# Latent attention layer: the probabilities' halves and the next tile's scaling queued between two halves of the filling, and the first head's units ahead of the second gate

## The chip, the cores and the metric

One core of a Trainium2 chip runs the whole program in one launch. The metric is the device time of one execution in microseconds (us). The kernel before takes 2921.37 us, the median of 3 runs (2921.25 to 2922.08).

## The reference

A decoder trunk of four residual layers on x of 1024 tokens by 1024 features, in float32: gated linear attention, multi-head latent attention (MLA), stick-breaking attention, gated linear attention, then a last RMSNorm. Only the MLA layer is touched by the change:

```python
proj = h @ w_in                      # c_q 256, c_kv 128, k_rope 64, gate g 2048
q = (rmsnorm(c_q) @ w_uq)            # 16 heads x (128 + 64 rotary)
kv = (rmsnorm(c_kv) @ w_ukv)         # 16 heads x (128 key + 128 value)
for i in range(8):                   # query tiles of 128 rows, all heads
    s = (q_nope[i] @ k_nope[:k_end].T + q_rope[i] @ k_rope[:k_end].T) * scale
    p = softmax(where(causal, s, -inf))          # k_end = 128 * (i + 1)
    o[i] = p @ v[:k_end]
y = (o * silu(g)) @ w_out            # 2048 -> 1024, added to x
```

## The kernel before, in words

**Numbers.** Every matrix product is made of three float16 products: each operand is split in a high half (ScalarE: a scaled copy to f16) and a low half (VectorE: the value less its high half). The stream x stays transposed in on-chip memory (xT, eight blocks of 128 features by 1024 tokens).

**Order.** A layer writes one list of items, `build_items` (L1047). Each engine's program goes through this list and issues its own share of every item (L454 to L480), so the list is the order of work on TensorE (PE), VectorE (DVE), ScalarE (ACT), GpSimd (POOL) and the SyncE queue (SP) alike. An engine waits at a semaphore for what it needs and everything of its own behind that waits with it.

**Items of one tile.** The 16 heads have 8 tiles each, t = 0 to 127, tile i of a head being i+1 blocks of 128 keys wide. For a tile t:

- `s` (L1154, PE): the scores, five products per 512 columns and one for the mask, in PSUM pair t mod 2. It waits for the low half of tile t-2 (L1164), which last used that pair.
- `m` (L1277 DVE, L1378 ACT): the row maximum of the scores, its negative, and on ACT the exponential with the row sum.
- `d` (L1290, DVE): the reciprocal of the row sum and the scaling of the probabilities in place.
- `t` (L1181, PE): i+1 transposes back to the PSUM pair. They wait for `d`.
- `e` (L1389 ACT, L1301 DVE): the high half of the transposed probabilities, then the low half.
- `pv` (L1188, PE): 3(i+1) products with the values. After every fourth tile DVE multiplies the result with the gate (yt, L1315), ACT makes its high half (L1403), POOL its low half (L1450).

In the list before, tile t+1's scores stand first and the filling stands behind `e`:

```python
main += [("s", t + 1)] if t < last else []
main += [("d", t)]
main += [("m", t + 1)] if t < last else []
main += [("t", t), ("e", t), ("gap", 1)]
main += [("pv", t - 1)] if t else []
```

**The filling.** At each ("gap", 1) the function `weave` (L45) puts in items of other work, in proportion to the cost of `pe_cost` (L996; 4 per product of 512 columns). A weave covers eight tiles: tile 7 of the head h-1 and tiles 0 to 6 of head h. Its filling is, in this order: the units of head h+1 (`head_items`, L1029), for an even h+1 first two rotary units of queries (qr) with their `rope` steps, then qn, qn, kn, kn, v, v; for h of 4 and more four output units (x), each cut in four parts; for h of 1 to 14 two gate units (g), each cut in four parts. So there are weaves with rotary units (h odd) and plain ones (h even). From head 4 on a weave's filling costs 528 (h odd) or 480 (h even).

What a finished unit leaves to other engines: qn, kn and v an ACT high half and a DVE low half (L443, L450); qr three DVE instructions (L1258, L1262 twice), a POOL sum, an ACT and a DVE half and 8 small DMAs by SP (L1478); x one DVE addition (L399); g the chain `gz` (L256): an ACT copy, a DVE clamp (L274), three ACT functions (L263, L265, L267), and at the item `g2`, behind the next unit, a DVE product (L280). `place_gates` (L1085) keeps `gz` at its place in the list here. The ACT half of a v unit waits until the products `pv` of the head before the last are done (L1360). Every slab of weights has one ACT and one DVE instruction for its halves (L182, L188), which `finish_items` (L142) puts ahead of the first unit of the slab before. Units take the PSUM banks 5, 6, 7 in turn, and a unit waits until the bank's last one is read.

**The start of the layer.** Behind the latent units come the gate of head 0, the gate of head 1 with the two `rope` steps of the keys in it, the units of head 0, and then `s` 0 and `m` 0. A `rope` step of queries makes SP issue 8 DMAs, which move the rotary halves to other partitions; `s` 0 waits for all 16 (L1161).

Of the kernel before, what the change touches and what calls it, by code (L numbers as in the profile page):

```python
# [44 lines left out]
def weave(main, filler, cost):  # L45

    total_weight = sum(item[1] for item in main if item[0] == "gap")
    total_cost = sum(cost(item) for item in filler)
    out, k, weight, spent = [], 0, 0, 0
    for item in main:  # L50
        if item[0] != "gap":
            out.append(item)
            continue
        weight += item[1]
        while k < len(filler) and (spent * total_weight < weight * total_cost):
            out.append(filler[k])
            spent += cost(filler[k])
            k += 1
    return out + filler[k:]
# [434 lines left out]
class StickBreaking:  # L494
# [112 lines left out]
    def build_items(self, w_in, w_out):  # L607
        L = self.L
        filler = L.cut(self.projections(0, w_in), ("q", "k", "v", "g"))
        first_gate = next(i for i, it in enumerate(filler) if it[0] == "part" and L.units[it[1]][0] == "g") - 1  # L610
        items = [("start",)] + filler[:first_gate] + [("z", 0), ("lh", 0), ("ll", 0), ("z", 1)]
        filler = filler[first_gate:]

        main = []
        for p in range(self.PAIRS):
            for i, step in enumerate(self.attention(p)):
                if i == self.SHIFT:
                    items += weave(main, filler, lambda it: it[0] in ("u", "part"))
                    filler = L.cut(self.projections(p + 1, w_in), ("q", "k", "v", "g")) if p + 1 < self.PAIRS else []
                    main = []  # L620
                main += step

        last = []
        for k in range(KD):
            last += L.slab(w_out[k], 1024, [("x", (k, c, True)) for c in range(2)], [5, 6, 7])
        early, last = L.open_early(L.cut(last, ("x",)), 2)
        items += weave(main, early, lambda it: it[0] == "part")
        items += [("pv", self.PAIRS * len(self.STEPS) - 1)] + last
        L.finish_items(items)
# [293 lines left out]
class LatentAttention:  # L923
# [123 lines left out]
    def build_items(self):  # L1047
        L = self.L
        latent = [self.add_slab(self.w["latent"][b], 1024, [("c", (b, c)) for c in range(2)]) for b in range(3)]
        items = [("start",)] + latent[0] + latent[1] + latent[2][:2] + [("sums", 0)] + latent[2][2:] + [("latent", 0)]  # L1050
        keys = self.add_slab(self.w["latent"][3], 1024, [("kr", (0, c)) for c in range(2)])
        items += keys[:2] + [("sums", 1)] + keys[2:] + [("latent", 1)]
        items += self.gate_items(0)
        ahead = self.gate_items(1)
        at = next(i for i, it in enumerate(ahead) if it[0] == "u") + 1
        items += ahead[:at] + [("rope", 0), ("rope", 1)] + ahead[at:] + self.head_items(0)
        last = MLA_HEADS * TT - 1
        items += [("s", 0), ("m", 0)]
        main, filler = [], []
        for t in range(last + 1):  # L1060
            h, i = divmod(t, TT)
            if i == 0:
                if h + 1 < MLA_HEADS:
                    filler += self.head_items(h + 1)
                if h >= self.GROUP:
                    filler += self.out_items(h // self.GROUP - 1, h % self.GROUP)
                if 1 <= h < MLA_HEADS - 1:
                    filler += self.gate_items(h + 1)
            if i == TT - 1:
                items += weave(main, L.cut(filler, ("x", "g")), self.pe_cost)  # L1070
                main, filler = [], []
            main += [("s", t + 1)] if t < last else []
            main += [("d", t)]
            main += [("m", t + 1)] if t < last else []
            main += [("t", t), ("e", t), ("gap", 1)]
            main += [("pv", t - 1)] if t else []
        items += [it for it in main if it[0] != "gap"]
        tail = []
        for part in range(4):
            tail += self.out_items(MLA_HEADS // self.GROUP - 1, part)  # L1080
        early, tail = L.open_early(L.cut(tail, ("x",)), 3)
        items += early + [("pv", last)] + tail
        L.finish_items(self.place_gates(items))
# [1098 lines left out]
```

How the kernel before makes its waits and increments, by code:

```python
    def load_slab(self, sp, s):  # L160
        if s >= len(self.slabs):
            return
        dram, cols = self.slabs[s]
        if s >= self.NLOAD:
            sp.wait_ge(self.w_lo_done, s - self.NLOAD + 1)
            sp.wait_ge(self.w_hi_done, s - self.NLOAD + 1)
        sp.dma_start(self.wf[s % self.NLOAD][:, 0:cols], dram).then_inc(self.w_loaded[s % self.NLOAD], 16)
# [8 lines left out]
    def act_w(self, act, s):  # L176
        cols = self.slabs[s][1]
        act.wait_ge(self.w_loaded[s % self.NLOAD], 16 * (s // self.NLOAD + 1))
        if s >= self.NSPLIT:
            act.wait_ge(self.acc_ready, self.last_unit_of[s - self.NSPLIT])
            act.wait_ge(self.w_lo_done, s - self.NSPLIT + 1)
        act.activation(self.w_hi[s % self.NSPLIT][:, 0:cols], self.wf[s % self.NLOAD][:, 0:cols],
                       ACT.Copy, scale=W_SCALE).then_inc(self.w_hi_done, 1)
# [1 line left out]
    def dve_w(self, dve, s):  # L185
        cols = self.slabs[s][1]
        dve.wait_ge(self.w_hi_done, s + 1)
        dve.scalar_tensor_tensor(out=self.w_lo[s % self.NSPLIT][:, 0:cols],
                                 in0=self.wf[s % self.NLOAD][:, 0:cols], scalar=W_SCALE,
                                 in1=self.w_hi[s % self.NSPLIT][:, 0:cols],
                                 op0=ALU.mult, op1=ALU.subtract).then_inc(self.w_lo_done, 1)
# [1 line left out]
    def wait_unit(self, eng, n):  # L193
        eng.wait_ge(self.acc_free[self.units[n][3]], self.turn[n])
# [86 lines left out]
    def wait_done(self, eng, n):  # L282
        eng.wait_ge(self.done, self.order.index(n) + 1)
```

## Time and profile before

| | |
|---|---|
| median of 3 runs | 2921.37 us |
| the profiled execution's own time | 2920.31 us |
| its span, first to last instruction | 2918.6 us |
| busy, whole span | PE 85%, PEld 49%, DVE 52%, ACT 44%, POOL 14% |
| mean granted TensorE clock | 0.944 |
| the latent layer | about 535 to 1580 us of the span |
| its attention, first scores to last transposes | 665 to 1532 us |

PE is busy over 85% of the span and every other engine for about half of it or less, so the time is read as the work of PE plus what PE waits for. The chain that ended last shows only the last normalization, 20 us at the end, and says nothing of this layer; the waits and the order of time inside the layer do.

### The profile page before, as it was taken

The numbers are of one execution on the slowest core, as the hardware profiler recorded it, in microseconds if no ns is written. First come the engines' busy times: TensorE is split into PE (matmuls) and PEld (weight loads), VectorE is DVE, ScalarE is ACT, GpSimd is POOL, SyncE is SP. The second block draws the span as 40 slices with busy tenths as digits, with TensorE's granted clock in tenths as the row PEclk, the third lists the DMA queues.
The fourth block names the chain that finished last, engine by engine and source line by source line (L and its number), as shares of the span: only waits on it lengthen the run. The fifth ranks groups of instructions, "written<-read, shape, count | busy, mean of one in ns | idle before, by whom it ended". The sixth has DMA issues, their size and how long they took to land. (4 is left out here: it accounts for less than half of the span.)

```text
span 2918.6 us, 43195 instructions
## 1 busy us (share of the span) xinstructions
PE 2487.2 (85%) x17616; PEld 1425.6 (49%) x17616; DVE 1518.8 (52%) x2167; ACT 1283.1 (44%) x1937; POOL 411.3 (14%) x300
## 2 busy tenths in 40 slices
PE   4999988686888988988886899999998779999977
PEld 1667643233545554554553455444454335665543
DVE  5455453455565565555554455555555434455543
ACT  3433332243443443344433477777777423334321
POOL 2000001220000001010003122222222230000001
PEclk9999999898999999999998899999999989999998
DMA  2111100101011010010100111111111001111002
GB/s 88 37 37 37 38 29 30 51 20 28 21 31 33 21 35 27 31 33 21 41 15 29 51 51 51 44 51 38 44 42 47 22 23 37 37 37 37 30 29 72
DMA packets 43032, 107.87 MB, mean 37 GB/s; under 512 B 7986, under 2 KB 13362, under 8 KB 42836
## 3 DMA queue, kind: packets, MB, share of 16 engines
q1 hardware_dynamic: 42836, 105.11, 11.7%
q8 instruction: 141, 2.31, 0.3%
q14 instruction: 55, 0.45, 0.0%
HBM read 84.11 MB, written 4.19 MB: 30 GB/s over the span
## 5 line engine op out<-in xcount | busy, mean ns | idle before, releaser
L1387 ACT ACTIVATE mla_prob<-psum,mla_neg_top 128x128 f32<-128x128 f32 (+7 forms) x128 | 94.5, 738 | 369.1 <-DVE mla_neg_top L1288 340.8
L219 PE MATMUL psum<-h_hi,gla_w_hi 128*128 128x512 f16 (+1 forms) x544 | 212.5, 391 | 41.7 <-DVE h_lo L377 41.7
L888 POOL TENSOR_TENSOR sb_al<-sb_zc,sb_ah 128x256 f16<-128x256 f32 (+2 forms) x96 | 166.2, 1731 | 419.8 <-ACT sb_ah L852 419.8
L220 PE MATMUL psum<-h_lo,gla_w_hi 128*128 128x512 f16 (+1 forms) x544 | 211.7, 389 | 0.0
L221 PE MATMUL psum<-h_hi,gla_w_lo 128*128 128x512 f16 (+1 forms) x544 | 210.9, 388 | 0.0
L1305 DVE TENSOR_TENSOR mla_pt_lo<-psum,mla_pt_hi 128x128 f16<-128x128 f32 (+7 forms) x128 | 97.0, 758 | 195.2 <-ACT mla_pt_hi L1395 195.2
L235 PE MATMUL psum<-gla_w_hi,h_hi 128*128 128x128 f16 x1024 | 173.8, 219 | 0.0
L236 PE MATMUL psum<-gla_w_lo,h_hi 128*128 128x128 f16 x1024 | 173.6, 219 | 0.0
L237 PE MATMUL psum<-gla_w_hi,h_lo 128*128 128x128 f16 x1024 | 173.6, 219 | 0.0
L1185 PE MATMUL psum<-mla_ident,mla_prob 128*128 128x128 f32 x576 | 90.1, 285 | 94.2 <-DVE mla_prob L1300 94.1
L219 PE MATMUL psum<-h_hi,sb_w_hi 128*128 128x512 f16 x384 | 151.1, 394 | 22.4 <-DVE h_lo L377 22.4
L399 DVE SCALAR_TENSOR_TENSOR xT<-psum,xT 128x512 f32<-128x512 f32 x112 | 77.1, 689 | 178.9 <-PE psum L221 178.8
L1284 DVE TENSOR_REDUCE mla_top<-psum 128x1 f32<-128x128 f32 (+7 forms) x128 | 96.7, 755 | 106.4 <-PE psum L1179 106.3
L220 PE MATMUL psum<-h_lo,sb_w_hi 128*128 128x512 f16 x384 | 151.1, 393 | 0.0
L221 PE MATMUL psum<-h_hi,sb_w_lo 128*128 128x512 f16 x384 | 150.7, 392 | 0.0
L219 PE MATMUL psum<-h_hi,mla_w_hi 128*128 128x512 f16 x320 | 124.8, 390 | 29.8 <-DVE h_lo L377 24.3
L759 DVE TENSOR_TENSOR sb_Ll<-sb_Lf,sb_Lh 128x256 f16<-128x256 f32 (+2 forms) x96 | 96.9, 1009 | 90.2 <-ACT sb_Lh L844 90.2
L1450 POOL TENSOR_TENSOR mla_y_lo<-mla_yt,mla_y_hi 128x512 f16<-128x512 f32 x32 | 37.0, 1156 | 688.9 <-ACT mla_y_hi L1403 688.9
L220 PE MATMUL psum<-h_lo,mla_w_hi 128*128 128x512 f16 x320 | 124.6, 389 | 0.0
L1185 PEld LDWEIGHTS psum<-mla_ident,mla_prob 128*128 128x128 f32 x576 | 66.9, 143 | 117.4 <-DVE mla_prob L1300 111.6
L221 PE MATMUL psum<-h_hi,mla_w_lo 128*128 128x512 f16 x320 | 124.2, 388 | 0.0
L829 ACT ACTIVATE sb_Lf<-sb_zc 128x256 f32<-128x256 f32 (+2 forms) x96 | 80.8, 842 | 95.6 <-DVE sb_zc L753 95.6
(316 smaller groups left out, 6951.3 us busy)
## 6 DMA issues: line engine op xcount, KB each, us to landing
sb_wf<-in_sb_in SPq DMA_DIRECT2D x32, 512.0 KB, 3.7
gla_wf<-in_gla_v SPq DMA_DIRECT2D x16, 512.0 KB, 3.5
gla_wf<-in_gla_g SPq DMA_DIRECT2D x16, 512.0 KB, 3.5
gla_wf<-in_gla_out SPq DMA_DIRECT2D x16, 512.0 KB, 3.4
mla_wf<-in_mla_gate SPq DMA_DIRECT2D x16, 512.0 KB, 3.4
mla_wf<-in_mla_out SPq DMA_DIRECT2D x16, 512.0 KB, 3.5
xT<-in_x_T SPq DMA_DIRECT2D x8, 512.0 KB, 6.5
gla_wf<-in_gla_q SPq DMA_DIRECT2D x8, 512.0 KB, 3.5
```

What stands on the lines that cost most here:

```text
L219: pe.matmul(out, wh[:, w], act_hi[:, k, tok], start=(i == 0), stop=False)
L220: pe.matmul(out, wh[:, w], act_lo[:, k, tok], start=False, stop=False)
L221: mm = pe.matmul(out, wl[:, w], act_hi[:, k, tok], start=False, stop=(i == last))
L235: pe.matmul(out, act_hi[:, k, tok], wh[:, w], start=(i == 0), stop=False)
L236: pe.matmul(out, act_hi[:, k, tok], wl[:, w], start=False, stop=False)
L237: mm = pe.matmul(out, act_lo[:, k, tok], wh[:, w], start=False, stop=(i == last))
L759: dve.tensor_tensor(self.Ll[s % 2][:, :, off:HALF], self.Lf[s % 2][:, :, off:HALF], self.Lh[s % 2][:, :, off:HALF], ALU.subtract).then_inc ...
L888: pool.tensor_tensor(self.al[s % 2][:, :, off:HALF], self.zc[s % 4][:, :, off:HALF], self.ah[s % 2][:, :, off:HALF], ALU.subtract).then_in ...
L1185: mm = pe.transpose(self.pair(t)[:, j * P:(j + 1) * P], self.prob[t % 2][:, j * P:(j + 1) * P], self.ident[:])
L1284: dve.reduce_max(self.top[:, k], self.pair(t)[:, 0:w], AX_X).then_inc(self.top_ready, 1)
L1305: dve.tensor_tensor(self.pt_lo[t % 2][:, 0:w], self.pair(t)[:, 0:w], self.pt_hi[t % 2][:, 0:w], ALU.subtract).then_inc(self.ptl_ready, 1)
L1387: act.activation(self.prob[t % 2][:, 0:w], self.pair(t)[:, 0:w], ACT.Exp, bias=self.neg_top[:, k], scale=self.SCALE, accum_out=self.total[ ...
```

## The change

The units of head 0 stand ahead of the second gate, the key's `rope` steps stand in the first gate, and `d` 0 stands behind `m` 0. In the tile loop `d` of a tile moves one tile ahead of its transposes, and the one gap becomes two, with `e` of this tile and `d` of the next between them. The number of gaps of a weave goes from 8 to 16, each worth half as much. No instruction is added or removed.

```diff
-        items += self.gate_items(0)
-        ahead = self.gate_items(1)
+        ahead = self.gate_items(0)
         at = next(i for i, it in enumerate(ahead) if it[0] == "u") + 1
-        items += ahead[:at] + [("rope", 0), ("rope", 1)] + ahead[at:] + self.head_items(0)
+        items += ahead[:at] + [("rope", 0), ("rope", 1)] + ahead[at:] + self.head_items(0) + self.gate_items(1)
         last = MLA_HEADS * TT - 1
-        items += [("s", 0), ("m", 0)]
+        items += [("s", 0), ("m", 0), ("d", 0)]
         main, filler = [], []
         for t in range(last + 1):
...
-            main += [("s", t + 1)] if t < last else []
-            main += [("d", t)]
-            main += [("m", t + 1)] if t < last else []
-            main += [("t", t), ("e", t), ("gap", 1)]
+            main += [("s", t + 1), ("m", t + 1)] if t < last else []
+            main += [("t", t), ("gap", 1), ("e", t)]
+            main += [("d", t + 1)] if t < last else []
+            main += [("gap", 1)]
             main += [("pv", t - 1)] if t else []
```

## Rows read from the trace of the kernel before

**Rows 1.** Busy time of the attention stretch: PE, PEld, DVE, ACT, POOL, clock, DMA

```profile
666.00:1544.00 878.00, 750.04 (x5375) 444.28 (x5373) 503.12 (x971) 355.46 (x681) 62.57 (x46) 0.95 0.09 28
```

**Rows 2.** Waits of PE, 666 to 1532 us: total, times, longest

```profile
PE psum L1185 <- DVE mla_prob L1300: 94.1, 50, 4.1
PE psum L1173 <- DVE mla_pt_lo L1305: 25.8, 27, 2.3
```

**Rows 3.** Timeline of PE at head ends: start, us, idle before, releaser

```profile
1037.01 0.48 PE L1185 MATMUL psum<-mla_ident,mla_prob 128*128 128x128 f32 x1 [4.08 <-DVE mla_prob L1300]
...
1047.14 0.44 PE L1185 MATMUL psum<-mla_ident,mla_prob 128*128 128x128 f32 x2 [1.60 <-DVE mla_prob L1300]
...
1076.90 0.38 PE L1173 MATMUL psum<-mla_kn_hi,mla_qn_hi 128*128 128x512 f16 x1
...
1085.75 1.09 PE L1185 MATMUL psum<-mla_ident,mla_prob 128*128 128x128 f32 x8 [1.21 <-DVE mla_prob L1300]
...
1091.09 0.27 PE L1173 MATMUL psum<-mla_kn_hi,mla_qn_hi 128*128 128x256 f16 x1
...
1093.31 0.33 PE L1185 MATMUL psum<-mla_ident,mla_prob 128*128 128x128 f32 x1 [1.46 <-DVE mla_prob L1300]
...
1103.09 0.44 PE L1185 MATMUL psum<-mla_ident,mla_prob 128*128 128x128 f32 x2 [3.57 <-DVE mla_prob L1300]
```

**Rows 4.** Busy time by stretches of 2 us, columns as in rows 1

```profile
1104.00:1106.00 2.00, 1.66 (x5) 0.59 (x5) 0.42 (x1) 0.67 (x3) 0.47 (x1) 0.51 0.05 12
```

**Rows 5.** Timeline of PE, SP and DVE at the layer's start

```profile
629.46 0.53 PE L219 MATMUL psum<-h_hi,mla_w_hi 128*128 128x512 f16 x1 [2.48 <-DVE mla_w_lo L188]
...
653.28 0.62 SPq L1478 DMA_DIRECT2D mla_qr_stack<-mla_st_hi  x1
...
662.96 0.59 SPq L1478 DMA_DIRECT2D mla_qr_stack<-mla_st_lo  x1
...
665.97 0.29 DVE L1284 TENSOR_REDUCE mla_top<-psum 128x1 f32<-128x128 f32 x1 [8.63 <-PE psum L1179]
```

**Rows 6.** Timeline of DVE at a plain head end

```profile
1082.81 1.09 DVE L1305 TENSOR_TENSOR mla_pt_lo<-psum,mla_pt_hi 128x896 f16<-128x896 f32 x1 [2.08 <-ACT mla_pt_hi L1395]
...
1084.41 0.42 DVE L274 TENSOR_SCALAR mla_gate_tmp<-mla_silu_g 128x512 f32<-128x512 f32 x1
...
1084.94 0.75 DVE L1300 TENSOR_SCALAR mla_prob<-mla_prob,mla_inv_total 128x1024 f32<-128x1024 f32 x1
...
1088.11 1.22 DVE L1305 TENSOR_TENSOR mla_pt_lo<-psum,mla_pt_hi 128x1024 f16<-128x1024 f32 x1 [2.03 <-ACT mla_pt_hi L1395]
1089.25 1.22 DVE L188 SCALAR_TENSOR_TENSOR mla_w_lo<-mla_wf,mla_w_hi 128x1024 f16<-128x1024 f32 x1
1090.39 0.68 DVE L450 SCALAR_TENSOR_TENSOR mla_qn_lo<-psum,mla_qn_hi 128x512 f16<-128x512 f32 x1
```

**Rows 7.** Timeline of ACT at the same head end

```profile
1084.87 0.63 ACT L263 ACTIVATE mla_gate_tmp<-mla_gate_tmp 128x512 f32<-128x512 f32 x1 [1.54 <-DVE mla_gate_tmp L274]
...
1087.07 1.01 ACT L1395 ACTIVATE mla_pt_hi<-psum 128x1024 f16<-128x1024 f32 x1
1087.97 1.05 ACT L182 ACTIVATE mla_w_hi<-mla_wf 128x1024 f16<-128x1024 f32 x1
1088.92 1.21 ACT L443 ACTIVATE mla_qn_hi<-psum 128x512 f16<-128x512 f32 x2
...
1098.69 1.08 ACT L443 ACTIVATE mla_v_hi<-psum 128x512 f16<-128x512 f32 x2 [3.66 <-PE psum L1203]
```

**Rows 8.** Timeline of DVE at a head end with rotary units

```profile
1029.55 0.68 DVE L1258 SCALAR_TENSOR_TENSOR mla_rt<-psum,mla_cos 128x512 f32<-128x512 f32 x1
1030.25 1.39 DVE L1262 SCALAR_TENSOR_TENSOR mla_rt<-psum,mla_sin 64x512 f32<-64x512 f32 x2
```

**Rows 9.** Timeline of ACT, tile 5 of a plain head

```profile
1073.04 1.01 ACT L1387 ACTIVATE mla_prob<-psum,mla_neg_top 128x896 f32<-128x896 f32 x1 [1.91 <-DVE mla_neg_top L1288]
...
1074.04 0.80 ACT L1395 ACTIVATE mla_pt_hi<-psum 128x768 f16<-128x768 f32 x1
```

## The prediction

> **What bounds the kernel now.** I read the page first (PE busy 85% of the span, no other engine much above half), then the busy time by stretches, then PE's waits, then the order of time around the longest of them. The attention stretch is 878 us long with PE busy for 750 [rows 1]. Nearly all the missing time is two waits: transposes that wait for the scaled probabilities (`t` for `d`), 94.1 us, and scores that wait for the low half (`s` for `e`), 25.8 us [rows 2]. The timeline shows where. Inside a head PE runs from item to item with no gap. It stands at head ends: 1.21, 1.46 and 3.57 us at a plain one, 4.08 and 1.60 us at one with rotary units [rows 3]. The reader is to see that `d` is late only because DVE serves it behind everything the filling left to it. After such a stand the granted clock is 0.51 of full, the level of 1.2 GHz, for some stretches [rows 4]; over the attention it is 0.95 [rows 1]. At the layer's start DVE waits 8.63 us for the first scores, while SP issues 16 DMAs from 653.28 to 663.55 [rows 5].
>
> **The start.** The rotary units' DMAs now run beside the second gate. Before, PE waited until 629.46 for the second gate's weight halves [rows 5] and then worked 10.4 us on it (48 products of 0.216). Now it takes the rotary units there, but head 0's own weight halves stand behind both gate chains on ACT, so PE stands some 5.6 us, at about 631 to 636.5. Behind that, rotary drains, halves and ropes on DVE run to about 645, `rope` 2 is ready at about 643.7 instead of 653.28, and its DMAs are issued until 654 and landed at 655.5. PE finishes the gate at 656.5 and starts the scores, 8.6 us before 665.1. The gate's chain (0.6 + 0.4 + three functions) is now ahead of the first exponential on ACT, so the first transposes come at 660.5 instead of 667.5. I take **-6.5 us**; bounds -8.6 (all of DVE's wait) and -3 (the stand at 631 turned into slow clock for the gate).
>
> **The loop, inside a head.** `e` now waits for the first half of the filling. For wide tiles PE has filling (3.3 us) and products (up to 1.2 us) to cover exponential, high half and low half; where only x parts and their one DVE addition lie in the first half, that cover holds and I cost it at nothing. If it were gone, `e` would cost PE its own 0.7 to 1.2 us per tile. Two places do not hold.
> (a) Gate chain in the first half. With cost 480 in 16 gaps of 30, gap 13 reaches for 390; the first gate unit ends at 384, so its chain `gz` goes into that same, odd gap, ahead of `e` of tile 5. Odd gaps are the ones before `e`. With 528 (33 a gap) gap 13 is full at 432, where the unit ends, and `gz` falls in gap 14, harmless. In the plain heads ACT finishes exp(6) at 1074.04 and now does the chain before the 0.80 us high half [rows 9]: 0.55 copy, 0.4 clamp, 2.0 functions put it at 1077.0 and the low half's end at 1078.7. PE, which started scores 7 at 1076.9 [rows 3], stands **1.8 us**, in six weaves (h = 4 to 14).
> (b) With rotary units, the gate slab's weight halves (1.05 ACT, 1.22 DVE, as in [rows 6, 7]) fall in gap 5 ahead of `e` of tile 1: 1.3 us.
>
> **A plain head end.** d(7) follows e(6) at once, at 1083.8; before, a gate product and the clamp stood between [rows 6]. Transposes 7 start 0.95 earlier, of the 1.21 of [rows 3]. But the clamp and so ACT's chain are 0.8 later: chain end and exp(0) at 1087.85. Ahead of hi(7) now stand the weight half (0.95 net) and two qn halves (1.2) [rows 7]: hi(7) is done at 1090.9 instead of 1088.0. DVE has its weight half, qn_lo, gate product and qn_lo ahead of e(7), which ends at 1093.0 instead of 1089.3 [rows 6]. Scores 1, which must wait for e(7), started at 1091.1 [rows 3]; now at 1093.0, transposes 0 end at 1093.8 against 1093.5. So **the stand of 1.46 becomes one of 3.4 at another semaphore, +0.3 us**. Next, the v halves on ACT wait for products 7 [rows 7], and hi(0), e(0), d(1) are now queued behind them: products 7 end at 1099.2, e(0) at 1101.35, transposes 1 end at 1102.5 against 1103.37, a stand of 2.1 for one of 3.57. That is 0.9 us won. The clock, however: the 3.4 us stand is as long as those that end at 0.5, and now the slow stretch lies on kn, v and x parts that release products 7. I charge 1.8 there and take back the 1.7 that the x parts pay now (their stretch at 0.51 [rows 4]). Result -0.8, then +1.8 for (a): **+1.0 us**. At h = 4, 8, 12 the fourth x part waits for POOL's low half of the head just finished, which is later than before behind d(1), a weight half and yt: +1.9 more, **+2.9**.
>
> **A rotary head end.** DVE is the bound there: each rotary unit leaves it 2.1 us (0.68 + 1.39) [rows 8]. Now w_lo, drain, gate product and drain stand before e(7), which ends at 1035.0; scores 1 start there and transposes 0 end at 1035.8, against 1037.3 [rows 3]. Then ropes, qn and kn halves reach e(0) at 1041.6, products 7 end at 1042.2 (a v unit waited 1.8 for its bank), transposes 1 end at 1043.4, or 1044.1 at the slow clock, against 1047.4 [rows 3]. So 3.3 us won, less 1.3 for (b): **-2.0 us**.
>
> **Heads 0 to 3 and 15** (no x, or only x): head 0 is bound by the chain through e, and three units in odd gaps put a half of 0.6 us into it, less one that is hidden: +1.5. Heads 1 and 3: the two rotary units fall in two different gaps, so e(7) stands behind one drain only: -3 each. Heads 2 and 15: 0.
>
> **Sum** against the profiled 2920.3: -6.5 + 1.5 - 2 x 3 - 5 x 2.0 + 3 x 1.0 + 3 x 2.9 = -9.3, so 2911. The median of the runs is 1.1 above the profiled execution: **2912 us**.
>
> The trace and a rule side by side: d(0) at rotary head ends starts only when DVE has ended the qn half in front of it, 4.08 us late for PE [rows 3]. The Trainium skill says the same as a general rule, that ACT's and DVE's queues are strictly in order while PE's can pull weight loads forward (TensorE: Matmul & The Clock Gate, Architectural detail). It speaks against this change, since it moves `e`, too, behind half of the filling; its time is the second rival's.
>
> **Rivals.**
> 1. The waits really go. For: 94.1 us wait for `d` alone, and `d` is now queued a whole tile earlier; it ends the slow clock too. Against: at head ends DVE and ACT, not the place of `d`, set the pace, and `e` joins the queue. If two thirds of 94.1 went, with 10 us of clock and the start: 2921 - 63 - 10 - 6 = 2842; if a third, 2921 - 31 - 5 - 6 = 2879. Chance 0.12.
> 2. Slower: the low half behind the filling. Place: the 14 head ends with filling ahead of e(7). Price: scores 1 wait for e(7) as at the plain head above, and the stand's slow clock falls on the units that release products 7 without the old slow stretch going; then each plain end costs 1.7 more and each rotary end 2 more than I took. 2912 + 7 x 1.7 + 7 x 2 = 2938. It decides from the point where the two stands after transposes 7 together exceed the old ones (5.0 plain, 5.7 rotary). Chance 0.27.
> 3. The loop nets nothing and only the start counts, 2914.9, or the start's gain goes as well because the DMAs, issued one by one, still end last: 2921. Chance 0.13 for the first, 0.05 for the second.
> My own case has 0.43.
>
> **Chances.** About 0.2% (5.8 us) is what a measurement of this kernel can tell from no change. My case, 2898 to 2920 by itself, is faster by more than that in about 0.33 of its 0.43; rival 1 always; half of the first part of rival 3. Slower by over 0.2% is rival 2 with a little of my case. Faster 0.52, same 0.21, slower 0.27. The range leaves out the far part of rival 1 and the end of rival 2: 2884 to 2936.
>
> **What would show it.** Right: PE's wait at the transposes falls from 94.1 to under 25, while its wait at the scores (for pt_lo) rises from 25.8 to 70 or more; first scores at 656 to 657; a stand of 2 or so before scores 7 in even heads from 4 on, none in odd ones; stands before scores 1 of 3 to 4 us, and the clock at half behind them. Wrong: a total of both waits under 60 us, a clock of 0.97 or more over the attention, or first scores later than 660.

## The result, and the profile after

The changed kernel takes 2926.14 us (median of 19 runs, 2922.43 to 2931.58) against 2919.99 us of the kernel before on the same chip (19 runs, 2912.11 to 2924.63). The ratio is 1.0024 with a 95% interval of 1.0018 to 1.0031: it is **slower by 0.24%**, where the forecast was 2912 us, faster by 0.3%. The profiled execution of after took 2923.05 us with a span of 2921.3 us. PE is busy for 85% of it, DVE for 52%, ACT for 44%, POOL for 14%, and the mean granted clock is 0.944: at this grain the page cannot be told from that of before. Of all runs in this document one, of experiment 9 at 6461.6 us, is more than twice as long as the others of its kernel and is left out of its ratio.

PE's waits can. The view is PE's waits between 655 and 1537 us of the kernel after, up to the last transposes as in [rows 2]: total, times, longest (L1172 is the first product of the scores, L1184 the transposes).

```profile
PE psum L1172 <- DVE mla_pt_lo L1304: 120.2, 65, 4.3
PE psum L1184 <- DVE mla_prob L1299: 9.6, 17, 3.1
```

Against [rows 2], 94.1 us at the transposes became 9.6, and 25.8 us at the scores became 120.2. The sum went from 119.9 to 129.8: for the 84.5 us that PE no longer waits for the scaling it waits 94.4 us more for the low half. The busy row of the attention, columns as in [rows 1], has the same clock of 0.95; PE is busy for 84.5% of it, against 85.4% in [rows 1]:

```profile
664.00:1550.00 886.00, 748.74 (x5364) 448.86 (x5365) 496.66 (x963) 350.30 (x674) 57.67 (x46) 0.95 0.09 27
```

**Where in the layer.** The latent layer, from its first Newton step (the first DVE step of its first normalization, L303; 540.26 us before, 536.76 after) to that of the next layer, is 1060.6 us long against 1051.6 before, +8.9. The way from that first step to the first transposes is 122.4 against 127.3, -4.9. The rest is by head: each head's time below is taken from the start of the transposes of tile 7 of the head before it to the start of its own (head 0 from its first transposes; PE's timeline has both).

| head | before, us | after, us | difference | forecast |
|---|---|---|---|---|
| 0 | 36.39 | 40.44 | +4.05 | +1.5 |
| 1 | 51.50 | 52.76 | +1.26 | -3 |
| 2 | 44.32 | 49.32 | +5.00 | 0 |
| 3 | 53.46 | 53.49 | +0.03 | -3 |
| 4, 8, 12 | 56.22, 56.00, 55.97 | 57.06, 60.51, 59.42 | +8.80 in all | +8.7 |
| 6, 10, 14 | 55.75, 55.74, 55.73 | 56.99, 56.29, 57.98 | +4.04 in all | +3 |
| 5, 7, 9, 11, 13 | 60.29, 60.30, 60.17, 60.25, 60.17 | 57.63, 57.62, 58.62, 57.88, 58.57 | -10.86 in all | -10 |
| 15 | 40.78 | 42.25 | +1.47 | 0 |

So heads 4 to 14 came out at +2.0 where the prediction's terms give +1.7, and heads 0 to 3 at +10.3 where they give -4.5. The same is seen in the waits. PE's waits up to 866 us, some 11 us into head 4 as the table counts it, first of the kernel before (from 665 us), then of the kernel after (from 655 us):

```profile
PE psum L1185 <- DVE mla_prob L1300: 19.5, 15, 2.7
PE psum L1173 <- DVE mla_pt_lo L1305: 16.7, 11, 2.3
```

```profile
PE psum L1172 <- DVE mla_pt_lo L1304: 45.6, 21, 4.3
PE psum L1184 <- DVE mla_prob L1299: 4.2, 5, 3.1
```

Both waits together are 36.2 us before and 49.8 us after in the first quarter of the layer. In the rest they are 83.7 before (119.9 less 36.2) and 80.0 after (129.8 less 49.8).

**The head ends after.** PE's timeline (start, us, idle before it, releaser) in one rotary head (its end of [rows 3] and scores 3 inside it) and in the plain head behind it (its end, and scores 7 inside it, the last line):

```profile
1037.48 0.28 PE L1172 MATMUL psum<-mla_kn_hi,mla_qn_hi 128*128 128x256 f16 x1 [3.47 <-DVE mla_pt_lo L1304]
...
1051.17 0.39 PE L1172 MATMUL psum<-mla_kn_hi,mla_qn_hi 128*128 128x512 f16 x1 [1.23 <-DVE mla_pt_lo L1304]
...
1084.48 1.09 PE L1184 MATMUL psum<-mla_ident,mla_prob 128*128 128x128 f32 x8 [0.27 <-DVE mla_prob L1299]
...
1092.88 0.28 PE L1172 MATMUL psum<-mla_kn_hi,mla_qn_hi 128*128 128x256 f16 x1 [2.90 <-DVE mla_pt_lo L1304]
...
1102.26 0.34 PE L1172 MATMUL psum<-mla_kn_hi,mla_qn_hi 128*128 128x384 f16 x1 [2.21 <-DVE mla_pt_lo L1304]
...
1106.35 0.61 PE L219 MATMUL psum<-mla_y_hi,mla_w_hi 128*128 128x512 f16 x1 [1.48 <-POOL mla_y_lo L1449]
...
1137.07 0.39 PE L1172 MATMUL psum<-mla_kn_hi,mla_qn_hi 128*128 128x512 f16 x1 [1.75 <-DVE mla_pt_lo L1304]
```

These are the stands the prediction walked through, at its places: 3.47 before scores 1 at a rotary end (3 to 4 forecast), 1.23 before scores 3 (1.3), 2.90 before scores 1 at a plain end (3.4), 2.21 behind the v halves (2.1), 1.48 for POOL's low half (1.9), and 1.75 before scores 7 (1.8), where the gate's chain lies ahead of the high half. DVE at the plain end, to be laid beside [rows 6]:

```profile
1083.67 0.76 DVE L1299 TENSOR_SCALAR mla_prob<-mla_prob,mla_inv_total 128x1024 f32<-128x1024 f32 x1
...
1088.67 1.23 DVE L188 SCALAR_TENSOR_TENSOR mla_w_lo<-mla_wf,mla_w_hi 128x1024 f16<-128x1024 f32 x1 [2.92 <-ACT mla_w_hi L182]
1089.82 0.68 DVE L450 SCALAR_TENSOR_TENSOR mla_qn_lo<-psum,mla_qn_hi 128x512 f16<-128x512 f32 x1
...
1091.62 1.21 DVE L1304 TENSOR_TENSOR mla_pt_lo<-psum,mla_pt_hi 128x1024 f16<-128x1024 f32 x1
```

Two executions are laid side by side by the start of transposes 7, 1085.75 before [rows 3] and 1084.48 here, since earlier parts of them differ too. The scaling now lets transposes 7 start after a stand of 0.27 us instead of 1.21, the 0.95 forecast. The low half of tile 7, which before stood ahead of the weight half, now stands behind it: it ends 8.35 us behind the start of transposes 7 (1092.83) instead of 3.58 (1089.33), 4.8 us later. The exchange can be read off these four lines.

**The clock** behind such a stand, by stretches of 2 us (columns as in [rows 1]), at this plain end and behind the longest stand of head 2:

```profile
786.00:788.00 2.00, 2.00 (x6) 0.76 (x5) 1.03 (x2) 0.63 (x1) 0.23 (x1) 0.50 0.00 0
...
1094.00:1096.00 2.00, 2.00 (x11) 1.11 (x10) 0.58 (x2) 0.89 (x3) 0.00 (x0) 0.50 0.00 0
...
1104.00:1106.00 2.00, 0.87 (x3) 0.00 (x0) 1.02 (x3) 1.54 (x4) 0.86 (x1) 0.50 0.52 131
```

At 0.50 of full the granted clock is the 1.2 GHz level. The prediction charged 1.8 us for a new slow stretch behind scores 1 and took back 1.7 for the old one of [rows 4], on the x parts. In this head both came: the stretch from 1104 us is at 0.50 still. Over the six plain heads of this execution, only head 10 has what was charged, the new one without the old. Heads 8 and 14 have both, and heads 4, 6 and 12 have only the one on the x parts.

### The profile page after: what moved, and what is told of

It reads as the page before. It is cut to its first block and busy times, and to the rows that moved or that the text cites. A ratio compares the mean times of both kernels' runs of the same rounds, so it can differ in the third digit from the quotient of the medians.

```text
span 2921.3 us, 43195 instructions
## 1 busy us (share of the span) xinstructions
PE 2483.2 (85%) x17616; PEld 1430.1 (49%) x17616; DVE 1513.6 (52%) x2167; ACT 1280.1 (44%) x1937; POOL 407.2 (14%) x300
## 5 line engine op out<-in xcount | busy, mean ns | idle before, releaser
L235 PE MATMUL psum<-gla_w_hi,h_hi 128*128 128x128 f16 x1024 | 173.8, 219 | 0.0
L1172 PE MATMUL psum<-mla_kn_hi,mla_qn_hi 128*128 128x512 f16 (+1 forms) x192 | 65.0, 338 | 120.7 <-DVE mla_pt_lo L1304 120.2
L829 ACT ACTIVATE sb_Lf<-sb_zc 128x256 f32<-128x256 f32 (+2 forms) x96 | 80.8, 842 | 94.4 <-DVE sb_zc L753 94.4
L766 DVE TENSOR_TENSOR sb_zc<-sb_zc,psum 128x256 f32<-128x256 f32 (+2 forms) x96 | 91.2, 950 | 52.3 <-PE psum L689 52.3
```

The lines of the kernel that those rows point to most:

```text
L235: pe.matmul(out, act_hi[:, k, tok], wh[:, w], start=(i == 0), stop=False)
L766: dve.tensor_tensor(zc, zc, net.psum[:, 2:4, off:HALF], ALU.subtract).then_inc(self.arg_ready, 1)
```

## The experiments

All runs are compared with the kernel before on their own chip, whose median was between 2919.5 and 2920.3 us. Diffs are against the changed kernel unless it is said otherwise.

**1 and 2. Which half of the change costs.** The changed start with the loop of before, and the loop alone with the start of before.

```diff
-        items += [("s", 0), ("m", 0), ("d", 0)]
+        items += [("s", 0), ("m", 0)]
...
-            main += [("s", t + 1), ("m", t + 1)] if t < last else []
-            main += [("t", t), ("gap", 1), ("e", t)]
-            main += [("d", t + 1)] if t < last else []
-            main += [("gap", 1)]
+            main += [("s", t + 1)] if t < last else []
+            main += [("d", t)]
+            main += [("m", t + 1)] if t < last else []
+            main += [("t", t), ("e", t), ("gap", 1)]
```

> The changed start of the layer with the tile loop of before. Theory L (the start wins about 6 us, the loop loses about 14, ten of them in the weaves of heads 0 to 3): first transposes 6 us earlier relative to the layer's start, all later head periods as before, time ratio to before 0.998 (2914 against 2920). Rival R (the start's gain is given back by slow clock and standing in head 0, the loop loses only 6 or 7, evenly): ratio 1.000.

```diff
-        ahead = self.gate_items(0)
+        items += self.gate_items(0)
+        ahead = self.gate_items(1)
...
-        items += ahead[:at] + [("rope", 0), ("rope", 1)] + ahead[at:] + self.head_items(0) + self.gate_items(1)
+        items += ahead[:at] + [("rope", 0), ("rope", 1)] + ahead[at:] + self.head_items(0)
```

> The changed tile loop with the start of before. Theory L: 2920 + 14 = 2934, ratio 1.0047. Rival R: 2920 + 7 = 2927, ratio 1.0024, the same as the whole change.

Measured: the start alone 2916.88 us, ratio 0.9996 [0.9987, 1.0006]; the loop alone 2932.89 us, 1.0052 [1.0038, 1.0066]. The loop alone costs 0.52%, about 15 us. The start alone cannot be told from no change, though in its profile the way to the first transposes is 122.42 us against 127.26, the same 4.8 us as after. Its profiled heads are those of before within 0.5 us each, so the loop is where the loss is. On the loop theory L's 1.0047 lies in the interval and the rival's 1.0024 does not; on the start it is the other way round, for L's 0.998 lies outside and the rival's 1.000 inside.

**3 and 7. Which heads.** The loop of before for heads 0 to 3 and the new one behind them, and the complement. Both have the changed start.

```diff
-        items += [("s", 0), ("m", 0), ("d", 0)]
+        items += [("s", 0), ("m", 0)]
...
-            main += [("s", t + 1), ("m", t + 1)] if t < last else []
-            main += [("t", t), ("gap", 1), ("e", t)]
-            main += [("d", t + 1)] if t < last else []
-            main += [("gap", 1)]
+            if (t + 1) // TT < 4:
+                main += [("s", t + 1), ("d", t), ("m", t + 1)]
+                main += [("t", t), ("e", t), ("gap", 1)]
+            else:
+                main += [("s", t + 1)] if t < last else []
+                main += [("d", t)] if t + 1 == 4 * TT else []
+                main += [("m", t + 1)] if t < last else []
+                main += [("t", t), ("gap", 1), ("e", t)]
+                main += [("d", t + 1)] if t < last else []
+                main += [("gap", 1)]
```

> The changed kernel, but the tiles up to the end of head 3 keep the old order and one gap; from tile 7 of head 3 on the new order. Theory L: the heads 0 to 3 give back their 10 us, time 2926 - 10 = 2916, ratio to before 0.9987 (start -6, heads 4 to 15 +3.5). Rival R: the loss is in every head, so at most a quarter of it comes back: 2924, ratio 1.0015.

```diff
-            main += [("s", t + 1), ("m", t + 1)] if t < last else []
-            main += [("t", t), ("gap", 1), ("e", t)]
-            main += [("d", t + 1)] if t < last else []
-            main += [("gap", 1)]
+            if (t + 1) // TT < 4:
+                main += [("s", t + 1), ("m", t + 1)]
+                main += [("t", t), ("gap", 1), ("e", t)]
+                main += [("d", t + 1), ("gap", 1)]
+            else:
+                main += [("s", t + 1)] if t < last else []
+                main += [("d", t)] if t + 1 > 4 * TT else []
+                main += [("m", t + 1)] if t < last else []
+                main += [("t", t), ("e", t), ("gap", 1)]
```

> The complement of the run with the old loop in heads 0 to 3: the new loop only up to the end of head 3, the old one behind it. Theory L: the heads 0 to 3 lose 10 us and heads 4 to 15 are as before: start -5, +10, time 2925, ratio to before 1.0017. Rival R (loss spread evenly): 2918, ratio 0.9993.

Measured: with the new order in heads 4 to 15 only, 2919.77 us, 1.0005 [0.9996, 1.0013], between the two numbers expected, so by itself it settles nothing. With the new order in heads 0 to 3 only, 2925.3 us, 1.0021 [1.0012, 1.0031], where the rival had 0.9993. Its heads 0 to 3 take 39.93, 53.54, 50.10 and 53.45 us, 197.0 in all against 185.7 before, and its heads from 5 on are those of before within 0.1 us. Head 4, where the two orders meet, takes 1.6 us more than before. Less the start alone (0.9996), the new order costs 0.25% (7.3 us) in four heads and 0.09% (2.6 us) in the twelve others. Each is the difference of two ratios that are known to about 0.1%, so the 0.25% is clear of zero and the 0.09% is not. The loss lies in the main in the quarter of the heads that has the least filling.

**4. The gate's chain.** A `gz` that falls between `t` and `e` is held back and put behind the next `d`.

```diff
-        L.finish_items(self.place_gates(items))
+        L.finish_items(self.place_gates(self.defer_gates(items)))
...
+    def defer_gates(self, items):
+        out, held, inside = [], [], False
+        for item in items:
+            if item[0] == "t":
+                inside = True
+            if inside and item[0] == "gz":
+                held.append(item)
+                continue
+            out.append(item)
+            if inside and item[0] in ("d", "pv"):
+                inside = False
+                out += held
+                held = []
+        return out + held
```

> The changed kernel, but a gate chain that falls into the first half of the filling is issued behind the low half and the next scaling. It touches head 2 (a stand of 4.1 us before scores 6 and a slow clock behind it) and heads 4, 6, ..., 14 (a stand of 1.75 us each before scores 7). Theory L: 4.5 + 6 x 1.75 = 15 us less than the changed kernel, 2911, ratio to before 0.997. Rival (the next thing in the queue is just as late, so that other stands take over half of it): 2918, ratio 0.9995.

Measured: 2912.37 us, 0.9978 [0.9969, 0.9986]; the chain's place is worth 0.46% (1.0024 less 0.9978), about 13 us. Theory L's 0.997 lies in the interval and the rival's 0.9995 outside. Scores 6 of head 2 in PE's timeline, first of the kernel after, then of this one:

```profile
785.77 0.53 PE L1172 MATMUL psum<-mla_kn_hi,mla_qn_hi 128*128 128x512 f16 x1 [4.14 <-DVE mla_pt_lo L1304]
```

```profile
786.37 0.39 PE L1187 MATMUL psum<-mla_kn_hi,mla_qn_hi 128*128 128x512 f16 x1 [1.20 <-DVE mla_pt_lo L1319]
```

Head 2 falls from 49.32 to 44.71 us (44.32 before), and the six plain heads from 4 to 14 together from 348.3 to 341.0: heads 8 and 12 by 3.1 and 2.0, and head 4 is 1.0 longer. The stand of 1.75 before scores 7 is gone there. ACT's timeline of the kernel after shows the 4.14 us being made:

```profile
780.34 0.90 ACT L1386 ACTIVATE mla_prob<-psum,mla_neg_top 128x768 f32<-128x768 f32 x1 [3.98 <-DVE mla_neg_top L1287]
...
781.23 0.59 ACT L261 ACTIVATE mla_silu_g<-psum 128x512 f32<-128x512 f32 x1
782.31 0.63 ACT L263 ACTIVATE mla_gate_tmp<-mla_gate_tmp 128x512 f32<-128x512 f32 x1 [0.49 <-DVE mla_gate_tmp L274]
782.97 0.63 ACT L265 ACTIVATE mla_gate_tmp<-mla_gate_tmp 128x512 f32<-128x512 f32 x1
783.63 0.63 ACT L267 ACTIVATE mla_gate_tmp<-mla_gate_tmp 128x512 f32<-128x512 f32 x1
784.17 0.69 ACT L1394 ACTIVATE mla_pt_hi<-psum 128x640 f16<-128x640 f32 x1
```

From the exponential's end the high half is 2.9 us away, of which the copy, the clamp's round trip and three functions take all. The low half ends at 785.7 and the scores start. The exponential's own 3.98 us of idle time says that ACT was not short of time; the order hurt.

**8. The rotary steps.** As experiment 4, but `rope` items are held and not `gz`.

```diff
-            if inside and item[0] == "gz":
+            if inside and item[0] == "rope":
```

(against experiment 4)

> The changed kernel, but a rope step that falls into the first half of the filling is issued behind the low half and the next scaling. In heads 1 and 3 the low half of tile 1 waited for the second rotary half on ACT, which waited for POOL, busy with the low half of the finished head: a stand of 4.3 us before scores 3. Theory L: these two stands shrink to under 2 us and the rotary head ends of heads 5 to 13 win up to 1 us each: 2926 - 2 x 3 - 5 x 0.7 = 2916.5, ratio to before 0.9988. Rival (the next unit's drain takes the place of the rope): 2925, ratio 1.0017.

Measured: 2925.69 us, 1.0023 [1.0013, 1.0033], which holds the rival's 1.0017 and not the theory's 0.9988: nothing is won. Scores 3 and scores 4 of head 1 in PE's timeline, first after, then here:

```profile
721.11 0.61 PE L1172 MATMUL psum<-mla_kn_hi,mla_qn_hi 128*128 128x512 f16 x1 [4.29 <-DVE mla_pt_lo L1304]
...
727.59 0.39 PE L1172 MATMUL psum<-mla_kn_hi,mla_qn_hi 128*128 128x512 f16 x1 [0.93 <-DVE mla_pt_lo L1304]
```

```profile
719.75 0.39 PE L1187 MATMUL psum<-mla_kn_hi,mla_qn_hi 128*128 128x512 f16 x1 [1.76 <-DVE mla_pt_lo L1319]
...
726.43 0.39 PE L1187 MATMUL psum<-mla_kn_hi,mla_qn_hi 128*128 128x512 f16 x1 [2.64 <-DVE mla_pt_lo L1319]
```

2.5 us go at scores 3 and 1.7 come back at scores 4. Heads 1 and 3 take 50.62 and 52.76 us, 2.1 and 0.7 less than after, and other heads of this profile give it back (head 4 alone takes 2.4 us more). So this run does not show that the rotary steps cost the kernel anything. The stand of 4.29 us itself is read from three engines in turn, POOL, ACT and DVE of the kernel after:

```profile
716.36 1.15 POOL L1449 TENSOR_TENSOR mla_y_lo<-mla_yt,mla_y_hi 128x512 f16<-128x512 f32 x1 [9.55 <-ACT mla_y_hi L1402]
717.47 1.26 POOL L1438 TENSOR_TENSOR mla_rt<-mla_rt 128x512 f32<-128x512 f32 x1
```

```profile
718.77 0.63 ACT L1376 ACTIVATE mla_st_hi<-mla_rt 128x512 f16<-128x512 f32 x1 [1.79 <-POOL mla_rt L1438]
```

```profile
719.43 0.69 DVE L1275 TENSOR_TENSOR mla_st_lo<-mla_rt,mla_st_hi 128x512 f16<-128x512 f32 x1 [3.16 <-ACT mla_st_hi L1376]
...
720.64 0.41 DVE L1304 TENSOR_TENSOR mla_pt_lo<-psum,mla_pt_hi 128x256 f16<-128x256 f32 x1
```

The rotary sum stands behind a y_lo on POOL, its high half behind that on ACT, its low half behind that on DVE, and the tile's own low half, 0.41 us of work, behind all of them.

**5 and 6. Both ahead of the filling.** If the low half was made late by being moved, it should go back ahead of the filling, with the new place of `d` kept: first with a gap between `e` and `d`, then with none.

```diff
-            main += [("t", t), ("gap", 1), ("e", t)]
+            main += [("t", t), ("e", t), ("gap", 1)]
```

> The changed kernel, but the halves of the probabilities stand ahead of all filling again, as before; only the next tile's scaling stays in the middle. Theory L (it is the low half behind the filling that costs): PE's wait at the scores falls from 120 to about 30 us; the scaling in the middle is still behind the drains of the first half, so part of the old wait at the transposes stays, 50 us or more. Time 2898, ratio to before 0.9925. Rival (the wait only belongs to whatever is queued last on DVE at a head end, so that the sum of the two waits stays about 120): time 2915, ratio 0.9985.

```diff
-            main += [("t", t), ("gap", 1), ("e", t)]
+            main += [("t", t), ("e", t)]
```

> The changed kernel, but halves and next scaling both stand ahead of one whole gap of filling. Theory L: nothing of the softmax waits behind filling of its own tile; wait at the scores about 30 us, at the transposes under 15; new stands of 1.5 to 2.8 us at kn, v or x units whose bank is drained late. Plain head ends 2.7 us shorter than before, rotary ones 4.4, start 5: 2920 - 5 - 7 x 2.7 - 7 x 4.4 = 2865, ratio 0.981. Rival (same sum of waits, moved to the banks of the units): 2915, ratio 0.9985.

Measured: 2905.65 us, 0.9956 [0.9944, 0.9969], and 2893.31 us, **0.9919 [0.9906, 0.9933]**, the fastest kernel of this study and faster than before and after. The theory's 0.9925 and 0.981 went too far, the rival's 0.9985 not far enough. In experiment 5 PE waits 31.0 us at the scores and 63.4 at the transposes (655 to 1545 us of its profile), as its theory said (about 30, and 50 or more): with the low half back ahead of the filling, PE's long wait for it is gone. PE's waits from 655 to 1535 us of the second kernel:

```profile
PE psum L1172 <- DVE mla_pt_lo L1304: 42.9, 37, 2.3
PE psum L219 <- DVE mla_w_lo L188: 23.7, 13, 2.8
PE psum L235 <- issue: 17.9, 15, 2.5
PE psum L219 <- POOL mla_y_lo L1449: 15.1, 4, 4.1
PE psum L219 <- issue: 12.0, 10, 1.8
PE psum L1184 <- DVE mla_prob L1299: 9.6, 17, 3.1
```

The two old waits are 52.5 us together, where before and after have 120 and 130. But 69 us of waits stand in places that had under 6 before: for weight halves, for POOL's low half, and "issue", where the trace names no releaser. One of each in PE's timeline:

```profile
1091.00 0.61 PE L219 MATMUL psum<-mla_y_hi,mla_w_hi 128*128 128x512 f16 x1 [4.14 <-POOL mla_y_lo L1449]
...
1133.77 0.39 PE L219 MATMUL psum<-mla_cq_hi,mla_w_hi 128*128 128x512 f16 x1 [2.75 <-DVE mla_w_lo L188]
...
1143.92 0.22 PE L235 MATMUL psum<-mla_w_hi,mla_ckv_hi 128*128 128x128 f16 x1 [2.46 <-issue]
```

A unit stands where the other engines have not caught up with the units before it; the product at L235 is the first of a v unit, and that it waits for its bank is argued from its place. The layer is 1030.8 us long, 20.8 less than before.

Most of the waits did not go but moved, as the rival said of their sum, though not of the time. From the first transposes to transposes 7 of head 15, all of PE's waits together are 118.5 us here, 125.1 before and 139.3 after. That stretch is 15.0 us shorter than before: PE stands still for 9.2 us less, and is busy for 732.1 us instead of 737.9, at a granted clock of 0.96 instead of 0.95. The start gives another 6.1 us.

**9. The products ahead of the filling too.** Would `pv` ahead of the gap release the v halves and POOL's y_lo sooner?

```diff
-            main += [("t", t), ("gap", 1), ("e", t)]
+            main += [("t", t), ("e", t)]
             main += [("d", t + 1)] if t < last else []
+            main += [("pv", t - 1)] if t else []
             main += [("gap", 1)]
-            main += [("pv", t - 1)] if t else []
```

> Halves and next scaling ahead of all filling, as in the run e6_e_d_first, and the products of the tile before ahead of the filling as well. Theory (what is left at head ends are drains that wait for the last tile's products: the v halves on ACT, and the POOL half that x parts need): the waits of PE for POOL fall from 15 us to under 7 and those put down to issue at kn, v and x units from 30 to under 15; heads 4 to 14 shorter by 1 to 2 us each; time 2880, ratio to before 0.987. Rival (the filling has to lie directly ahead of the products, else the scores of the next tile meet DVE with a full queue): 2893 or more, ratio 0.992 or more.

Measured: 2917.3 us, 0.9993 [0.9983, 1.0002]: the theory's 0.987 fell, and the rival (0.992 or more) stands. PE's waits for POOL went from 15.1 us to 2.7, as the theory said, but those put down to issue rose from 29.9 to 64.5, where it had under 15. Plain heads take 53.5 us, where experiment 6 has 57.1 to 57.3 in heads 4, 8 and 12 and 53.1 in heads 6, 10 and 14; rotary heads take 62.6, 3 to 4 more than there and 2.4 more than before. PE's and then ACT's timeline at a rotary end:

```profile
1043.94 0.27 PE L235 MATMUL psum<-mla_w_hi,mla_ckv_hi 128*128 128x128 f16 x1 [7.34 <-issue]
```

```profile
1041.50 0.63 ACT L1376 ACTIVATE mla_st_hi<-mla_rt 128x512 f16<-128x512 f32 x1 [2.48 <-POOL mla_rt L1438]
```

The last y_lo of the finished head has moved ahead of the rotary sums on POOL (it ends at 1040.25, and ACT's half waits for the sum behind it), and PE stands 7.34 us at a unit behind them. That the one causes the other is argued from the order, since the trace names no releaser there.

**10. What the start is worth.** Experiment 6 with the start of before (its `d` 0 still behind `m` 0).

> The run e6_e_d_first with the start of before. If the start's gain of about 5 us does not depend on the loop behind it: 2893 + 5 = 2898, ratio to before 0.9935. If it is given back in this loop: 2893, ratio 0.992.

Measured: 2904.2 us, 0.9948 [0.9935, 0.9960], so beside the better loop the start is worth 0.0029 of 2920, some 8.5 us (the two intervals leave room for 3 to 14), and the loop of experiment 6 by itself wins 0.52%, as much as the changed loop by itself costs. Of the two numbers expected, 0.9935 is at the edge of the interval and 0.992 outside. In the profiles the way to the first transposes is 121.20 us with it and 128.25 without, 7.1 us. Beside the changed loop it is worth 0.28% (1.0052 less 1.0024) and beside the old one 0.04%, with an interval from a gain of 0.13% to a loss of 0.06%.

## Why the prediction was wrong

**The step that failed** is the term for the first heads: "head 0 is bound by the chain through e ... +1.5", "Heads 1 and 3 ... -3 each", "Heads 2 and 15: 0". For heads 0 to 3 it gave -4.5; they came out at +10.3 in the profile, a miss of 14.8 us, and by timed runs at +7.3 (experiments 1 and 7), 11.8 off, of the 16.3 between the forecast's -9.3 and the measured +7.0 (0.24% of 2920). The terms were set down without a walk through the new order, while heads 4 to 14, which had one, came out within 0.3 us in sum. (The same order ran in them in the profiles of experiments 2 and 3, at +3.6 and +3.3 us against before.)

Under it lies a reading that was too wide: "Inside a head PE runs from item to item with no gap. It stands at head ends". That is so in heads 4 to 14 of the kernel before, but for waits of 0.6 us or less. It is not so in the first heads and in head 15. In head 0 PE stood before five scores in turn for the low half, two of them:

```profile
683.50 0.39 PE L1173 MATMUL psum<-mla_kn_hi,mla_qn_hi 128*128 128x512 f16 x1 [1.64 <-DVE mla_pt_lo L1305]
...
695.39 0.39 PE L1173 MATMUL psum<-mla_kn_hi,mla_qn_hi 128*128 128x512 f16 x1 [2.02 <-DVE mla_pt_lo L1305]
```

Of the 25.8 us of this wait before, 16.7 lie ahead of 866 us. Head 0 had no cover to spend, and the change puts more work ahead of the low half there.

What the walk would have shown is in three places.

- **Head 2** has the stand of (a), and worse. Its filling is 288 of cost in 16 gaps of 18; gap 11 reaches for 198, the first gate unit ends at 192, so `gz` goes in front of `e` of tile 4. I had worked (a) for h = 4 to 14 alone. There 30 of cost, 1.6 us of PE's work at 0.216 us per 4, and the products cover a part; here 18, or 1.0 us, do, and the tiles are narrower. The price was 4.14 us instead of 1.8, and a half-clock stretch behind it, +5.0 in all. Experiment 4 shows this cause alone: in its profile head 2 gets back 4.6 of the 5.0.
- **Heads 1 and 3** were to gain at e(7). They have a `rope` step ahead of `e` inside the head, where its low half comes through POOL, and the stand of 4.29 us before scores 3 of either head (in head 3 with 3.04 before scores 1 as well) takes the gain. This is read from the timelines; experiment 8 takes back 2.1 and 0.7 us in these heads of its profile, and nothing in its timed runs, so it is not shown by a run.
- **Head 0** waits 1.65 to 2.82 us before six scores, where before it waited 1.64 to 2.33 before five. Filling there is about 7 of cost a gap, under 0.4 us, so whatever stands ahead of `e` on ACT or DVE is paid in full. I had charged three halves and hidden one; +4.05 instead of +1.5. This was not isolated by a run of its own.

**Point by point.** *What bounds the kernel*: right, the waits of PE; and "the reader is to see that `d` is late only because DVE serves it behind everything the filling left to it" holds, for experiment 6, which puts `d` and `e` ahead of the filling, cuts the two waits to 52.5 us and wins 0.81%, some 24 us with the start. *The start, -6.5*: right in kind and 1.6 too large in the profile (-4.9). By timed runs the start alone gave 1.2 us, 5.3 short of the term and the second largest part of the miss; beside the changed loop it gave 8. The stand it foresaw at 631 to 636.5 us is there, 5.05 us long (5.6 forecast):

```profile
634.36 0.61 PE L219 MATMUL psum<-mla_cq_hi,mla_w_hi 128*128 128x512 f16 x1 [5.05 <-DVE mla_w_lo L188]
```

and the last of SP's DMAs of queries is issued at 652.40 instead of 662.96 [rows 5]; this layer began 3.5 us earlier in this profile, so 7.1 of the 10.6 are the change's. *(a) and (b)*: right in place and size where they were worked (1.75, 1.23). *Head ends*: their stands are right within 0.5 us each in the heads shown. *The clock*: mis-sized, for the old slow stretch, for whose end 1.7 us a plain head were taken back, stayed in five heads of six, and the new one came in three. Heads 8 and 12 lost 4.5 and 3.5 us and head 4 lost 0.8, with the same order of items; their sum, 8.8, fits the 8.7 of the prediction by luck. *Head 15*: +1.5 instead of 0; PE now stands 3.05 us before its scores 1, where before 0.75 and 0.38 went at two transposes.

**The rivals.** The first, that the waits really go, had the right engine in view and the wrong change: their sum rose by 9.9 us. The second is the nearest in time (2926 between my 2912 and its 2938) and in mechanism: the low half behind the filling. Its place was only partly right. It named the 14 head ends, with its price at plain and rotary ends. The rotary ends behaved as in my own case. Of the plain ones head 8 paid the rival's price (4.5 us, its 2.9 + 1.7), with both slow stretches as it said, and the six together did not (12.8 us, where my case has 11.7 and the rival 21.9). The price was paid inside heads 0 to 3 in the main, and inside the even heads by the gate's chain. The rule that ACT's and DVE's queues are strictly in order (the Trainium skill, TensorE: Matmul & The Clock Gate, Architectural detail), which the prediction set against the change, is borne out: PE's wait for the low half went from 25.8 to 120.2 us.

**What would show it, as it came**: the wait at the transposes under 25 (9.6) and at the scores 70 or more (120.2); a stand of 2 before scores 7 in even heads from 4 on (1.75), none in odd ones (none). The stands before scores 1 are 3.47 us at rotary ends, with the clock at half behind them, and 2.30 to 2.90 at plain ones, where 3 to 4 was said, with the clock at half behind three of the six. The first scores end at 656.2, since the first maximum starts there:

```profile
656.18 0.28 DVE L1283 TENSOR_REDUCE mla_top<-psum 128x1 f32<-128x128 f32 x1
```

That lies in the 656 to 657 forecast only because this layer began 3.5 us earlier: counted from the layer's first step the first maximum is 6.3 us earlier than before (119.4 against 125.7), where 8.6 was forecast. None of the signs for "wrong" came, and the time went the other way all the same. Every sign was taken from heads that had been walked through, from the start or from a total, and none from heads 0 to 3.

**What stays open.** Why the start alone wins 1.2 us by the ratio and 2.6 by the medians, with 4.8 in its profile, and 8.5 beside the loop of experiment 6, was not settled. The first layer, which the change does not touch, varies by up to 5 us between profiled executions, more than the thing to be explained. Nor was the clock's share of each head parted from that of the waits, and heads 0, 1 and 3 were not isolated by a run that shows in the time.

## What to carry to other kernels

Where one list sets the order of every engine, what PE waits for next belongs ahead of all filling on the in-order engines, and all of it: `d` moved forward at the price of `e` moved back only exchanged one wait for another (120 against 130 us), while both ahead of the filling won 0.52% by themselves and 0.81%, some 24 us, with the new start. Even so the waits mostly moved to the units, so look at the sum of all waits and at the clock, and not only at the two waits aimed at. Walk the windows with the least filling by themselves: the same gate chain cost a stand of 1.75 us where half of a tile's filling is 1.6 us of PE's work, and 4.14 where it is 1.0. When gaps are made finer, work out anew which chain falls in which gap, as the gate chains that fell in an odd gap, one in each of seven heads, cost 13 us here.

## What the runs showed of the hardware beyond this

- The stand before scores 1 is followed at once by a stretch at 0.50 in head 8 and not at the same place in head 6, in one execution with the same order of items. There the clock falls only later, on the x parts (0.50 from 988 to 990 us). The stand in head 6 in PE's timeline, and the stretches before and behind it, columns as in [rows 1]; the clock, third from the end, stays at 1.00:

```profile
978.28 0.28 PE L1172 MATMUL psum<-mla_kn_hi,mla_qn_hi 128*128 128x256 f16 x1 [2.90 <-DVE mla_pt_lo L1304]
```

```profile
976.00:978.00 2.00, 0.00 (x0) 0.00 (x0) 2.00 (x3) 0.41 (x1) 0.00 (x0) 1.00 0.20 66
978.00:980.00 2.00, 1.72 (x17) 1.31 (x18) 1.66 (x6) 0.23 (x1) 0.00 (x0) 1.00 0.00 0
980.00:982.00 2.00, 1.51 (x23) 1.20 (x21) 0.69 (x1) 0.82 (x3) 0.00 (x0) 1.00 0.00 0
```

  The stand is 2.90 us long in both heads.

- The untouched first layer brings the latent layer's first Newton step to 535.4 us in one profiled execution and to 540.9 in another, at a mean clock of 0.94 to 0.97 over the profiles of this study. Comparing one profile's layer with another's needs its own starting point, and parts of a few microseconds need the timed runs as well.
